# Reading the moving operand and writing the sums from the last column to the first, in two groups of matmuls

## What is computed

```
# first block
up = h @ ffn_w_up                        # 1024 -> 2 * 3072
gate, val = split(up)
gate = causal_depthwise_conv(gate, ...)
x = x + (gelu(gate) * val) @ ffn_w_down  # 3072 -> 1024
# second part, twice in each of two layers
x = x + scale * norm((silu(h @ w_gate) * (h @ w_up)) @ w_down)   # 1024 -> 2816 -> 1024
```

## Time and profile before

| what | value |
|---|---|
| median of three runs | 1470.13 us |
| the profiled execution's own time | 1472.22 us |
| its span in the trace | 1470.4 us |
| TensorE's mean granted clock | 0.997 |
| TensorE busy | 1443.3 us, 98% |
| VectorE busy | 966.4 us, 66% |
| ScalarE busy | 736.2 us, 50% |

### The profile page before, as it was taken

The page is one execution under the profiler, slowest core; times in us unless marked ns, Lnnn a source line. Parts: engine busy times, 40 slices in busy tenths (PEclk is TensorE's granted clock), DMA queues, the critical chain, the costliest instruction groups (busy, mean ns, idle before and its releaser), DMA issues. The chain is left out here.

```text
span 1470.4 us, 21371 instructions
## 1 busy us (share of the span) xinstructions
PE 1443.3 (98%) x8920; PEld 1269.0 (86%) x8920; DVE 966.4 (66%) x1163; ACT 736.2 (50%) x936; POOL 90.8 (6%) x106
## 2 busy tenths in 40 slices
PE   7999999999999999999999999999999999999998
PEld 7899999899998788888987888878888898788886
DVE  5867786687874666555886666556655578766644
ACT  5533853555543544445655444445444567544432
POOL 0000000000000000000540000000000036000000
PEclk9999999999999999999999999999999999999999
DMA  7735455676655477554524765556754473365542
GB/s 244 248 115 173 141 185 191 166 192 174 188 184 198 143 234 239 174 198 132 153 91 131 223 192 184 175 186 214 229 193 153 149 189 108 116 214 179 192 153 105
DMA packets 251412, 259.14 MB, mean 176 GB/s; under 512 B 26659, under 2 KB 213428, under 8 KB 251316
## 3 DMA queue, kind: packets, MB, share of 16 engines
q1 hardware_dynamic: 250432, 255.49, 55.1%
q10 hardware_dynamic: 884, 2.28, 0.4%
HBM read 256.69 MB, written 1.05 MB: 175 GB/s over the span
## 5 line engine op out<-in xcount | busy, mean ns | idle before, releaser
L1000 DVE TENSOR_TENSOR w_lo<-raw,w_hi 128x2048 fp32r<-128x2048 f32 x240 | 546.0, 2278 | 321.3 <-ACT w_hi L606 321.1
L606 ACT ACTIVATE w_hi<-raw 128x2048 fp32r<-128x2048 f32 x240 | 456.2, 1901 | 337.7 <-PE psm L1678 155.5
L1678 PE MATMUL stream<-a_hi,w_hi 128*128 128x256 f32 x1072 | 307.5, 287 | 2.7 <-DVE a_lo L1019 1.5
L1678 PE MATMUL stream<-a_hi,w_lo 128*128 128x256 f32 x1072 | 304.6, 284 | 0.0
L1678 PE MATMUL stream<-a_lo,w_hi 128*128 128x256 f32 x1072 | 304.5, 284 | 0.0
L1678 PE MATMUL stream<-w_hi,a_hi 128*128 128x512 f32 (+1 forms) x576 | 225.4, 391 | 8.2 <-DVE w_lo L1000 5.8
L1678 PE MATMUL stream<-w_hi,a_lo 128*128 128x512 f32 (+1 forms) x576 | 221.3, 384 | 0.0
L1678 PE MATMUL stream<-w_lo,a_hi 128*128 128x512 f32 (+1 forms) x576 | 221.0, 384 | 0.0
L1678 PEld LDWEIGHTS stream<-a_hi,w_hi 128*128 128x128 f32 x1072 | 206.9, 193 | 5.0 <-issue 2.9
L1678 PEld LDWEIGHTS stream<-a_lo,w_hi 128*128 128x128 f32 x1072 | 207.0, 193 | 0.1
L1678 PEld LDWEIGHTS stream<-a_hi,w_lo 128*128 128x128 f32 x1072 | 206.9, 193 | 0.0
(11 more groups left out here) (291 smaller groups left out, 1725.5 us busy)
## 6 DMA issues: line engine op xcount, KB each, us to landing
raw<-in_ffn_w_up SPq DMA_DIRECT2D x136, 512.0 KB, 5.0
raw<-in_ffn_w_down SPq DMA_DIRECT2D x104, 512.0 KB, 4.4
raw<-in_ffn_w_gate SPq DMA_DIRECT2D x88, 512.0 KB, 4.0
raw<-in_w_in SPq DMA_DIRECT2D x80, 512.0 KB, 4.7
raw<-in_w_out SPq DMA_DIRECT2D x24, 512.0 KB, 4.4
raw<-in_w_ret_o SPq DMA_DIRECT2D x8, 512.0 KB, 4.0
raw<-in_w_lru_o SPq DMA_DIRECT2D x8, 512.0 KB, 4.2
diag<-in_conv_diag SPq DMA_DIRECT2D x8, 512.0 KB, 5.7
```

Of the source, the lines that this page charges most:

```text
L606: nc.scalar.activation(w_hi[s][:, :, 0:n], raw[s][:, :, 0:n], ACT.Copy).then_inc(w_hi_ready, 1)
L1000: V.tensor_tensor(w_lo[s][:, :, 0:n], raw[s][:, :, 0:n], w_hi[s][:, :, 0:n].bitcast(F32), ALU.subtract).then_inc(w_split, 1)
L1678: return nc.tensor.matmul(dst, lhs, rhs, start=start, stop=stop, skip_group_check=True)
```

## The change

Two functions get a parameter order, a function that is put on the moving operand and on the destination. Its default leaves them as they are; in the up projection of the first feed-forward and in all down projections it is backward, which reverses the columns of both. The stationary operand, the order of the matmuls, their number and all waits stay.

```diff
+            def backward(ap):
+                return ap[:, ::-1]
...
-                        to = dst[:, at:at + T]
+                        to = order(dst[:, at:at + T])
...
-                        mm(to, lhs(w_hi[s], k), hi_t[:, k, :], begin, False)
-                        mm(to, lhs(w_hi[s], k), lo_t[:, k, :], False, False)
-                        ins = mm(to, lhs(w_lo[s], k), hi_t[:, k, :], False, end)
+                        mm(to, lhs(w_hi[s], k), order(hi_t[:, k, :]), begin, False)
+                        mm(to, lhs(w_hi[s], k), order(lo_t[:, k, :]), False, False)
+                        ins = mm(to, lhs(w_lo[s], k), order(hi_t[:, k, :]), False, end)
...
-                    mm(dst, hi_t[:, k, tok], h[:, n, :], begin, False)
-                    mm(dst, hi_t[:, k, tok], l[:, n, :], False, False)
-                    ins = mm(dst, lo_t[:, k, tok], h[:, n, :], False, end)
+                    mm(order(dst), hi_t[:, k, tok], order(h[:, n, :]), begin, False)
+                    mm(order(dst), hi_t[:, k, tok], order(l[:, n, :]), False, False)
+                    ins = mm(order(dst), lo_t[:, k, tok], order(h[:, n, :]), False, end)
...
             for j in range(NF1):
-                project(U1_UP + j, G1_UP + j, stream[(G1_UP + j) % 3], a_hi, a_lo, a_ready(N_UP1, 1) if j == 0 else None)
+                project(U1_UP + j, G1_UP + j, stream[(G1_UP + j) % 3], a_hi, a_lo, a_ready(N_UP1, 1) if j == 0 else None,
+                        order=backward)
...
-                    wide_pass(c, t, y_bank(t, n), h_hi, h_lo, ks, first, last)
+                    wide_pass(c, t, y_bank(t, n), h_hi, h_lo, ks, first, last, order=backward)
```

More of the change, by code:

```diff
@@ L1687, in end_pass, with feature_major @@
                 ins.then_inc(unit_used, 1)
-            def feature_major(s, dst, tiles, hi_t, lo_t, first, last, kts=range(KT), ready=None):
+            def feature_major(s, dst, tiles, hi_t, lo_t, first, last, kts=range(KT), ready=None, order=lambda ap: ap):
                 for n, (lhs, at) in enumerate(tiles):
@@ L1723, in token_major, with wide_pass @@
                 return ins
-            def wide_pass(c, t, dst, hi_t, lo_t, ks, first, last, ready=None):
+            def wide_pass(c, t, dst, hi_t, lo_t, ks, first, last, ready=None, order=lambda ap: ap):
                 split_unit(c)
@@ L1809, in _, with project @@
             spin(stream[1], 14)
-            def project(c, g, bank, hi_t, lo_t, ready=None, between=None):
+            def project(c, g, bank, hi_t, lo_t, ready=None, between=None, order=lambda ap: ap):
                 split_unit(c)
                 bank_free(g)
-                feature_major(c % NS, bank, BOTH[0:1], hi_t, lo_t, True, False, ready=ready)
+                feature_major(c % NS, bank[:, :], BOTH[0:1], hi_t, lo_t, True, False, ready=ready, order=order)
                 if between:
                     between()
-                end_pass(feature_major(c % NS, bank, BOTH[1:2], hi_t, lo_t, False, True), c)
+                end_pass(feature_major(c % NS, bank[:, :], BOTH[1:2], hi_t, lo_t, False, True, order=order), c)
             for u in range(8):
```

## The result

| | before | changed |
|---|---|---|
| median | 1470.13 us (1469.91 to 1472.45) | 1476.87 us (1476.33 to 1479.00) |
| ratio | | 1.0042, 95% interval 1.0031 to 1.0053 |
| profiled execution, span | 1472.22, 1470.4 us | 1476.87, 1475.0 us |

A forecast was written before the change was run, and what follows sets the result against it. TensorE was taken to bound the kernel, by number of matmuls times pitch in the changed stretches. The terms summed to 0 against the profiled 1472.22 us, given as a median of 1470.1 us, range 1437 to 1503.

The forecast's parts named there:

- What bounds the kernel: Up and down projections: TensorE alone, time is number of matmuls by pitch, 0.1200 and 0.2268 us, together 443 us.
- No instruction, wait, queue or evacuation changes: Whole kernel: nothing removed or added, queues see the same waits, readers of banks start as before; cost 0.
- The stream itself, taken at 0: Changed up and down projections: reading and writing backwards costs 0, bounded between 33.2 us less and 376 us more.
- The fixed part of 13.3 ns: Each matmul in the up and down projections: 13.3 ns of the pitch that doesn't depend on its columns.
- B: Rival: in 2496 up and down matmuls a small cost at the turn, up to 13.3 ns each, 33 us; chance 0.13.
- C: Rival: in the same matmuls the exposed turn gets shorter, at most 33 us less, 1437 us; chance 0.15.
- its 0.52: Whole kernel: chance given to no difference within 0.2%, 1467.2 to 1473.1 us, the forecast's case.
- Rival A, half rate: Up and down projections: backward streams pass at half rate, 376 us more, 1846 us; chance 0.20.
- The test "equal at 256 and 512 is a turn, twice as much a rate": Up and down pitches: growth equal in both forms means a turn's cost, twice as much at 512 a rate.
- Rival D: Whole kernel: the pattern is made forward again on the way to the chip, forecast's time; chance inside the 0.52.

The follow-up runs named there:

- The placed kernels: Kernel before, all forward, a_hi and a_lo laid 192 or 64 bytes further where they move: 1455.17 us (0.9900) and 1458.73 us (0.9927).
- either part alone: Changed kernel with the reversal kept in the down projections only: ratio 1.0059; in the first up projection only: 0.9985.
- The run by columns: Separate kernel of float32r matmul blocks, 128 to 512 columns, forward and backward: 120.0 against 118.3 ns at 256, 226.7 against 233.3 at 512.
- the bfloat16 runs: Matmul blocks without the model's work, in bfloat16 instead of float32r, forward and backward: 109.2 ns at 256 columns and 215.8 at 512.
- the blocks: Kernels without the model's work, 24 float32r matmuls a block, moving operand's place varied: forward 113.3 to 120.0 ns at 256 columns over sixteen places.

## Why the prediction was wrong

- *What bounds the kernel*: right. TensorE's stretches have no idle time after the change either, both parts added up to the measured total, and the changed distances account for the time of every kernel with a reversal. (The placed kernels gained less than their count of matmuls allowed, as said above.)
- *No instruction, wait, queue or evacuation changes*: right. The one wait ahead of the up projection's first matmul is still 1.05 us, and the write's direction costs nothing (1.0001).
- *The stream itself, taken at 0*: this is the step that failed. The figures were -1.7 ns (256) and +6.7 ns (512). I argued that the same addresses are read and that buffers and banks made no difference within 1 ns. But all of the rows that I compared had their operands at the same place against each other, a multiple of 256 bytes apart. They could not show that the place counts, and reversing the read changes the place at which each stream begins. I took the evenness of one layout for a property of the engine. (the earlier trace rows show psm and ps only; that the sums in stream cost the same with 512 columns holds in the trace, but not by those rows.)
- *The fixed part of 13.3 ns*: I read it rightly as an exposed part of each matmul, but not rightly as independent of the columns: forward it is 13.3 ns at 256, 320, 384 and 512 columns, 15.7 at 448, and at 128 and 192 the columns don't set the distance at all (111.7 ns). Rivals B and C put the effect there, with a bound of 13.3 ns that held for both forms. Their error was to expect one sign for both forms. What happened is C at 256 columns and B at 512, and their net is 7.0 us where each alone was given up to 33. The range held the result because the bound on one matmul held; either part alone (8.7 us more, 2.2 less) would lie in it too. That the total moved as little as 0.4% is luck in part: the two signs cancel, and no step foresaw that. The forecast and its 0.52 didn't hold.
- *Rival A, half rate*: refuted, the distances moved by 1 to 3%.
- *The test "equal at 256 and 512 is a turn, twice as much a rate"*: too poor. The run by columns shows a third shape, a pattern that goes up and down with the number of columns.
- *Rival D*: refuted by the same distances.

What stays open: why certain places and lengths are better. The runs show that the exposed part depends on the moving operand's place against the stationary one, on the number of columns, on the direction and, off the multiples of 256 bytes, on what ran before. Two reads of SBUF that get in each other's way at the turn would fit that, but no run shows them, and it is only argued. The Trainium skill says in "TensorE: Matmul & The Clock Gate", Part 2, that the moving operand and the weight load have read ports of their own and that loading weights takes no bandwidth from the running matmul. Nothing in the bfloat16 runs speaks against it (109.2 and 215.8 ns in either direction, at one place). In float32r the figures depend on how the two lie against each other, which that rule alone doesn't lead one to expect; no run here shows whether the ports are the reason.

## What to carry to other kernels

In a kernel bound by float32r matmuls, the distance between starts, worked out to a tenth of a nanosecond from a few dozen rows, is the number to watch: 1 to 7 ns in each of thousands of matmuls is the whole effect, and the placing of the moving tile against the stationary one within 256 bytes moved it more than the direction did. For 256 moving columns try a few offsets that are no multiple of 256 bytes (in the blocks 64, 112, 144 and 192 gave the least, once each; in the kernel 192 and 64 did, 1.0 and 0.7% faster), and read the distance in every stretch, since the same offset gave 113.3 and 117.8 ns in one trace; for 512 keep both on the same place and read forward. When a prediction rests on "the same in every row", ask first in what all those rows are alike.

## What was unexpected of the hardware

- A matmul of 256 float32r columns at the full clock lay between 113.3 and 125.0 ns from the next in the steady part of a block, with the same work; one of 512 columns between 226.7 and 240.0.
- Below a length the columns stop counting: 128 and 192 columns both took 111.7 ns with a new stationary operand each time.
- In bfloat16 the same blocks took 109.2 and 215.8 ns, with no trace of the direction (the place was not varied); the exposed part is 2.5 ns there (109.2 - 106.7, and 215.8 - 213.3) and 6.7 to 26.7 in float32r.
- A layout's figure can depend on what ran before: with the activations 192 bytes off, projections of one trace with the same tiles lay 117.8 ns apart (114.06 to 118.30 us) and 113.3 (182.29 to 186.37 us). At multiples of 256 bytes no such second level was seen: forward, 120.0 ns in every one of those blocks.
